# Residual updates of a SwiGLU down projection: by VectorE out of PSUM, in place of ScalarE copies and accumulating DMAs

## The chip, the cores and the metric

The kernel runs on one core of one Trainium2 chip. The metric is the device time of one launch in microseconds (us). The engines are named TensorE (PE in the profile), VectorE (DVE), ScalarE (ACT), GpSimd (POOL) and SyncE (SP). Each has its own instruction queue, worked through in order; semaphores tie the queues together. PEld is TensorE's weight load, which overlaps the matmul before it. PSUM has eight banks of 512 fp32 columns on 128 partitions.

## What is computed

One decoder layer on x (256 tokens, 2048 channels), fp32. Cut to what matters here:

```python
def swiglu(h, w_gate, w_up, w_down):
    return (jax.nn.silu(h @ w_gate) * (h @ w_up)) @ w_down

x = x + 0.5 * swiglu(rmsnorm(x, norm_ffn1), w1_gate, w1_up, w1_down)   # D_FF = 5632
h = rmsnorm(x, norm_mix); z = h @ w_in
x = x + concat(o_mla(z), o_rwkv(z)) @ w_out       # attention and RWKV-7 heads
x = x + 0.5 * swiglu(rmsnorm(x, norm_ffn2), w2_gate, w2_up, w2_down)
x = x + sigmoid(rmsnorm(x, norm_ple) @ w_ple_gate) * (p @ w_ple_proj)
```

The change touches the two SwiGLU blocks (f = 0 and f = 1).

## The kernel before

Every fp32 product is made of three fast products: each operand is split into a high part and the remainder, and hi\*hi, hi\*lo and lo\*hi are summed in PSUM. For a weight block `n` (1 MB, `raw[n % 3]`), ScalarE rounds it to `whi[n % 3]` (`split_hi`, L422), then VectorE subtracts to get `wlo[n % 2]` (`split_lo`, L431). SyncE loads block n + 3 into the same `raw` slot once `wlo` of block n is written (`load_unit`, L405, for gate and up; `load_block`, L396, for down).

A SwiGLU block goes through its 5632 hidden columns in 11 groups of 512. Ten passes (i = 0 to 9) each work on 12 weight blocks, numbered here u0 to u7 and d0 to d3:

- u0 to u7 are gate and up products for the next group of columns (`pe_units`). The even ones are plain products (L538 to L540, 24 matmuls). The odd ones use a seven-product scheme for the gate, which needs sums of weights `T` (`weight_forms` on VectorE, L443, L446, L448), their high part `t_hi` (`forms_hi` on ScalarE, L453) and their low part `t_lo` (`forms_lo` on VectorE, L458); 21 matmuls each (L555 to L557).
- d0 to d3 are the down products of the group that is ready (`down`, L471 to L473): four chunks of 512 output columns, 24 matmuls each, chunk j into banks 2j and 2j + 1. A pass has 4\*24 + 4\*21 + 4\*24 = 276 matmuls.
- At the end of the u blocks VectorE combines the gate and up sums (`combine_gate`, L801 to L808; `combine_up`, L813, L816), ScalarE applies silu (L676), VectorE makes h (`hidden`, L822) and turns it in quads (`h_turn`, L830). h then makes a trip through DRAM (`store_h`, `load_hT`) and comes back transposed for the next pass's down products.

The order on each engine is written out by hand: `pe_pass`, `act_pass`, `dve_pass` go through 12 steps s, and each step lists what stands in it. In `dve_pass`, step 9 ends with `split_lo` of d2, step 10 with `split_lo` of d3, step 11 has `split_lo` of the next pass's u0 and then `weight_forms` of the next u1. Passes 1 to 8 run as a hardware loop (L661, L780, L938); pass 9 stands behind it, and a last group of down products behind that.

The result of chunk j leaves PSUM so. ScalarE copies the two banks, times 0.5, into a buffer `xs[j % 2]` (`down_out`, L722) in steps 9, 10, 11 and, for chunk 3, step 0 of the next pass. GpSimd then issues a DMA that adds `xs` to `x` (`pool_add_x`, L1437), 80 in all. `xs` has two buffers, so the copy of chunk j waits for the add of chunk j - 2 (`x_added`). Before the next pass uses the banks, TensorE waits for the copies: `pe_pass` waits for chunk 2 before the first product (L634), `pe_units` for chunk 3 before the thirteenth (L568). The eleventh group's four chunks are added straight from the banks by VectorE (`last_out`, `update_x`, L850).

Of the kernel before, what the change touches and what calls it, by code (L numbers as in the profile page):

```python
# [11 lines left out]
ALU = mybir.AluOpType  # L12
ACT = mybir.ActivationFunctionType
# [3 lines left out]
P = 128  # L17
# [143 lines left out]
def hybrid_layer(nc, table, w, out):  # L161
    where = constant_table()[1]
    ctx = ExitStack()
    with ctx:
# [62 lines left out]
        t_hi = sb("t_hi", [P, WEIGHT_FORMS, COLS], F32R)  # L227
        more_hi = sb("more_hi", [P, SEVEN, 3 * P], F32R)
        more_lo = sb("more_lo", [P, SEVEN, 3 * P], F32R)
        XS0 = base[0]  # L230
        xs = sb("xs", [P, 2, TT, COLS])
        tok = sb("tok", [P, TT, TOKEN_FORMS, P], at=XS0)
        h_quads = sb("h_quads", [P, 4, FKT, TT, 32])


# [111 lines left out]
        h_dram = nc.dram_tensor("h_scratch", [P, TT * COLS], F32, kind="Internal").ap()  # L347
        tok_ready, tok_hi, tok_lo = map(sem, ("tok_ready", "tok_hi", "tok_lo"))
        p_done, s1_ready, combined = map(sem, ("p_done", "s1_ready", "combined"))
        x_evac, x_added = sem("x_evac"), [sem(f"x_added{k}") for k in range(2)]  # L350
        vec, pool_chain, zero_row = sem("vec"), sem("pool_chain"), sem("zero_row")
        z_evac, lora_stored, zero_stored = sem("z_evac"), sem("lora_stored"), sem("zero_stored")
        z_stored, z_shifted = sem("z_stored"), sem("z_shifted")
# [205 lines left out]
        def pe_units(pe, f, i, it):  # L559

            n = FFN_BASE[f] + PAIRS + 12 * i
            for v in range(PAIRS):
                m = n + v
                pe.wait_ge(lo_ready, m + 1 + 12 * it)
                if v % 2 == 0:
                    for out in (OUT_11, OUT_21, OUT_12, OUT_22):
                        if v == 0 and out == OUT_12 and i:
                            pe.wait_ge(x_evac, evacs(f, i - 1, 3) + 4 * it)  # L568
                        for kk in range(2):
                            ins = eight_products(m, out, kk, v == 0 and kk == 0, v == 6 and out == OUT_22 and kk == 1)  # L570
                    ins.then_inc(block_used, 1)
                    continue
                first, last = v == 1, v == 7
                if (i, v) == (0, 1):
                    pe.wait_ge(h_ready, NFF * f + 1)
                if i == 0:
                    pe.wait_ge(tok_lo, SEVEN * f + pair_of(m) + 1)
                ins = seven_product(m, P1, False, first, last)
                if last:
                    ins.then_inc(p_done, 1)  # L580
# [17 lines left out]
        def down(pe, f, i, it=0, last=False, turn_next=False):  # L598
            n = FFN_BASE[f] + PAIRS + 12 * i + (0 if last else PAIRS)
            h_hi, h_lo = (last_hT_hi, last_hT_lo) if last else (hT_hi, hT_lo)  # L600
            for j in range(4):
                if j == 0:
                    pe.wait_ge(hT_ready, NFF * f + i + 1 + it)
                if turn_next and j == 2:
                    pe.wait_ge(x_evac, evacs(f, i, 0))
                    last_h_turn(pe, f)
                if last:
                    if j < 2:
                        pe.wait_ge(x_evac, evacs(f, i - 1, 2 + j))
                    else:  # L610
                        pe.wait_ge(banks_read, (READ_OUT, READ_GATE)[f] - 4 + j - 1)
                    banks = (4 + 2 * (j % 2), 5 + 2 * (j % 2))
                else:
                    if j == 0:
                        pe.wait_ge(s1_ready, (NFF - 1) * f + i + 1 + it)
                    pe.wait_ge(combined, steps(f, i, (1, 2, 4, 5)[j]) + 5 * it)
                    banks = (2 * j, 2 * j + 1)
                products(pe, n + j, h_hi, h_lo, range(FKT), [banks], COLS, True, True, it)
                if last and j >= 2:
                    turn_x(pe, 2 * f + 1, (2 * j - 4, 2 * j - 3))  # L620
# [10 lines left out]

        def pe_pass(pe, f, i, it=0, turn_next=False):
            if i:
                pe.wait_ge(x_evac, evacs(f, i - 1, 2) + 4 * it)  # L634
            pe_units(pe, f, i, it)
            down(pe, f, i, it, turn_next=turn_next)

# [75 lines left out]
            act.wait_ge(p_done, 4 * ((NFF - 1) * f + i) + 1 + 4 * it)  # L713
            nc.scalar.activation(s1[:, :], PS[:, 0, :], ACT.Copy).then_inc(s1_ready, 1)

        def down_out(act, f, i, j, it=0):

            act.wait_ge(block_used, FFN_BASE[f] + PAIRS + 12 * i + PAIRS + j + 1 + 12 * it)
            adds = 2 * ((NFF - 1) * f + i) + j // 2
            if adds:  # L720
                act.wait_ge(x_added[j % 2], 16 * adds + 32 * it)
            nc.scalar.activation(xs[:, j % 2, :, :], PS[:, 2 * j:2 * j + 2, :], ACT.Copy, scale=0.5).then_inc(x_evac, 1)  # L722

        def token_hi(act, f, p):

            act.wait_ge(tok_ready, SEVEN * f + p + 1)
# [13 lines left out]
        def act_pass(act, f, i, it=0, turn_next=False):  # L740

            n = FFN_BASE[f] + PAIRS + 12 * i
            for s in range(12):
                if s == 0 and i:
                    down_out(act, f, i - 1, 3, it)
                if s in (0, 2, 4, 6):
                    forms_hi(act, n + s + 1, it)
                if s == 7:
                    first_sum(act, f, i, it)
                if s == 8:  # L750
                    silu(act, f, i, it)
                if s >= 9:
                    down_out(act, f, i, s - 9, it)
                split_hi(act, n + s + 2, it)
                if s == 4:
                    hT_part_hi(act, f, i, it)
                if s == 3 and not i:
                    token_hi(act, f, 3)
                if i == 0 and s in (1, 2):
                    (store_h, load_hT)[s - 1](act, f, 0)  # L760
                if not turn_next and s in (9, 10):
                    (store_h, load_hT)[s - 9](act, f, i + 1, it)
                if turn_next and s == 10:
                    last_hT_part_hi(act, f)

        def act_ffn(act, f, B):
# [13 lines left out]
            with act.Fori(0, NFF - 3) as it:  # L780
                act_pass(act, f, 1, it)
            act_pass(act, f, NFF - 2, turn_next=True)
            down_out(act, f, NFF - 2, 3)
            for s in range(4):
                split_hi(act, B + FFN_BLOCKS - 4 + s + 2)
            xT_parts_hi(act, 2 * f + 1, range(4))
# [56 lines left out]
            nc.vector.tensor_tensor(last_hT_lo[:, :, :].rearrange(banks, b=2), PS[:, 0:2, :],  # L843
                                    f32(last_hT_hi[:, :, :]).rearrange(banks, b=2), ALU.subtract).then_inc(hT_ready, 1)

        def update_x(dve, n, j, factor, it=0):

            dve.wait_ge(block_used, n + 1 + 12 * it)
            b = 4 + 2 * (j % 2)
            nc.vector.scalar_tensor_tensor(x[:, :, j * COLS:(j + 1) * COLS], PS[:, b:b + 2, :], factor,  # L850
                                           x[:, :, j * COLS:(j + 1) * COLS], ALU.mult, ALU.add).then_inc(banks_read, 1)

        def last_out(dve, f, B, j):
            dve.wait_ge(x_added[j % 2], 32 * (NFF - 1) * (f + 1) - 16 * (j < 2))
# [34 lines left out]
        def dve_pass(dve, f, i, it=0, turn_next=False):  # L889

            n = FFN_BASE[f] + PAIRS + 12 * i
            for s in range(12):
                if s == 8:
                    combine_up(dve, f, i, it)
                if i or s:
# [13 lines left out]
                if s == 8:  # L909
                    hidden(dve, f, i, it)  # L910
                    if not turn_next:
                        h_turn(dve, f, i + 1, it)
                if turn_next and s == 10:
                    last_hT_part_lo(dve, f)

        def dve_ffn(dve, f, B):
# [510 lines left out]
            pool_tt(pool, zst[:, :, :], zst[:, :, :], pvst[:, :, :], ALU.add)  # L1427
            pool.dma_start(z_dram[1:SEQ + 1, c:c + COLS].rearrange("(t p) c -> p t c", p=P), zst[:, :, :]).then_inc(z_stored, 16)

        def pool_add_x(pool, f):  # L1430

            for i in range(NFF - 1):
                for j in range(4):
                    pool.wait_ge(x_evac, evacs(f, i, j))
                    if i:
                        pool.wait_ge(x_added[j % 2], 16 * (2 * ((NFF - 1) * f + i - 1) + j // 2 + 1))
                    pool.dma_start(x[:, :, j * COLS:(j + 1) * COLS], xs[:, j % 2, :, :], accum_op=ALU.add).then_inc(  # L1437
                        x_added[j % 2], 16)

        def pool_aux(pool):  # L1440

            pool.wait_ge(con_loaded, 16)
# [2 lines left out]
            pool.dma_start(z_dram[0, :].rearrange("(p c) -> p c", p=P), zeros[:, :]).then_inc(zero_stored, 16)  # L1445
            pool.wait_ge(var_ready, 1)
            power(rstd[:, 0:2], "minus_half", rstd_ready)
            pool_add_x(pool, 0)
# [790 lines left out]
        def _(pool):  # L2239
# [10 lines left out]
            for k in range(2):  # L2250
                pool.wait_ge(var_ready, 5 + k)
                power(rstd[:, 4 + 2 * k:6 + 2 * k], "minus_half", rstd_ready)
                if k == 0:
                    pool_add_x(pool, 1)

        @block.tensor
        def _(pe):
# [93 lines left out]
        def _(dve):  # L2351
# [5 lines left out]
            for j in range(4):  # L2357
                for s in range(4):
                    if 4 * j + s >= 2:
                        split_lo(dve, WOUT + 4 * j + s + 1)  # L2360
                    if 4 * j + s == 9:
                        dve.wait_ge(p_hi, 1)
                        nc.vector.tensor_tensor(hT_lo[:, 0:2, :], PS[:, 0, :].rearrange("p (k s) -> p k s", k=2), f32(hT_hi[:, 0:2, :]),
                                                ALU.subtract).then_inc(p_ready, 1)
                update_x(dve, WOUT + 4 * j + 3, j, 1.0)
            split_lo(dve, PROJ + 1)
            xT_parts_lo(dve, 2, range(2))
            split_lo(dve, PROJ + 2)
# [47 lines left out]
```

## Time and profile before

| | us |
|---|---|
| median of 3 runs | 2008.17 (2005.13 to 2008.56) |
| profiled execution, its time | 2011.02 |
| profiled execution, its span | 2009.2 |
| PE busy | 1968.8 (98%) |
| DVE busy | 1522.9 (76%) |
| ACT busy | 1069.9 (53%) |
| POOL busy | 235.4 (12%) |

The profile is one execution; 1.8 us of its time lie outside the span. Busy shares are averages over the whole program. The granted TensorE clock was 0.997 of full speed.

### The profile page before, as it was taken

How to read it: one execution, taken by the hardware profiler on the slowest of the kernel's cores; microseconds unless marked ns; L12 is line 12 of the kernel's file. 1: busy time of each engine (PE TensorE's matmuls, PEld its weight loads, DVE VectorE, ACT ScalarE, POOL GpSimd, SP SyncE). 2: the span in 40 equal slices, each digit the busy share in tenths (PEclk: the TensorE clock that was granted, in tenths of full speed). 3: DMA queues.
4: the chain of work that ended last, by engine and by line, in shares of the span. 5: the costliest groups of instructions: out<-in, count | busy, mean ns of one | idle time of the engine just before them, and what ended most of it. 6: DMA issues, size and time to landing. Idle time of an engine off the chain costs nothing.

```text
span 2009.2 us, 28838 instructions
## 1 busy us (share of the span) xinstructions
PE 1968.8 (98%) x11016; PEld 1619.8 (81%) x11016; DVE 1522.9 (76%) x1364; ACT 1069.9 (53%) x1043; POOL 235.4 (12%) x190
## 2 busy tenths in 40 slices
PE   8999999999999999999898999999999999999999
PEld 6778778888888889888777888778887888887887
DVE  5978888788787855756788547977888888887664
ACT  4655555555554555855344346555555555555553
POOL 0000000000000000344533000000000000000000
PEclk9999999999999999999999999999999999999999
DMA  7688788877888766667312555688877888788854
GB/s 248 210 253 242 233 250 254 251 238 235 257 261 252 224 178 221 195 188 228 119 45 71 173 188 169 217 261 253 250 233 227 271 251 241 238 251 252 242 176 147
DMA packets 229035, 436.67 MB, mean 217 GB/s; under 512 B 12806, under 2 KB 32898, under 8 KB 228956
## 3 DMA queue, kind: packets, MB, share of 16 engines
q1 hardware_dynamic: 189116, 361.48, 53.7%
q0 software_dynamic: 25440, 53.09, 13.4%
q10 hardware_dynamic: 14400, 20.98, 3.1%
q8 instruction: 57, 0.93, 0.2%
q14 instruction: 22, 0.18, 0.0%
HBM read 374.42 MB, written 16.00 MB: 194 GB/s over the span
## 4 chain that ended last, share of the span: by engine, by line
PE 79%; DVE 10%; DMA 7%; ACT 2%; issue 2%; SPq 0%; DVEq 0%; ACTq 0%
PE PS L471 13%; PE PS L472 13%; PE PS L473 13%; DMA raw<-in_w_gate 7%; PE PS L538 6%; PE PS L540 6%; PE PS L539 6%; PE PS L555 5%; PE PS L556 5%; PE PS L557 5%; PE PS L1684 3%; DVE wlo L431 3%; DVE t_lo L458 2%; ACT t_hi L453 2%; DVE T L443 1%
## 5 line engine op out<-in xcount | busy, mean ns | idle before, releaser
L431 DVE TENSOR_TENSOR wlo<-raw,whi 128x2048 fp32r<-128x2048 f32 (+2 forms) x338 | 733.1, 2169 | 265.6 <-PE PS L473 246.2
L422 ACT ACTIVATE whi<-raw 128x2048 fp32r<-128x2048 f32 (+2 forms) x338 | 603.5, 1791 | 256.5 <-PE PS L473 143.8
L538 PE MATMUL PS<-whi,xT_hi 128*128 128x512 f32 x768 | 302.5, 394 | 5.0 <-issue 3.2
L540 PE MATMUL PS<-whi,xT_lo 128*128 128x512 f32 x768 | 300.5, 391 | 0.0
L539 PE MATMUL PS<-wlo,xT_hi 128*128 128x512 f32 x768 | 299.6, 390 | 0.0
L471 PE MATMUL PS<-whi,hT_hi 128*128 128x512 f32 x680 | 267.7, 394 | 1.5 <-DVE G L801 1.0
L473 PE MATMUL PS<-whi,hT_lo 128*128 128x512 f32 x680 | 265.0, 390 | 0.0
L472 PE MATMUL PS<-wlo,hT_hi 128*128 128x512 f32 x680 | 264.9, 390 | 0.0
L453 ACT ACTIVATE t_hi<-T 128x2048 fp32r<-128x2048 f32 x80 | 153.4, 1917 | 196.6 <-DVE T L448 196.6
L1437 POOL DMA_DIRECT2D x_resid<-xs x80 | 96.1, 1202 | 1195.2 <-ACT xs L722 1168.8
L458 DVE TENSOR_TENSOR t_lo<-T,t_hi 128x2048 fp32r<-128x2048 f32 x80 | 183.3, 2292 | 53.0 <-ACT t_hi L453 53.0
L471 PE MATMUL PS<-whi,xT_hi 128*128 128x512 f32 (+2 forms) x536 | 206.3, 385 | 0.0
L473 PE MATMUL PS<-whi,xT_lo 128*128 128x512 f32 (+2 forms) x536 | 203.4, 379 | 0.0
L472 PE MATMUL PS<-wlo,xT_hi 128*128 128x512 f32 (+2 forms) x536 | 203.3, 379 | 0.0
L722 ACT ACTIVATE xs<-PS 128x1024 f32<-128x1024 f32 x80 | 82.2, 1028 | 205.9 <-PE PS L473 142.1
L538 PEld LDWEIGHTS PS<-whi,xT_hi 128*128 128x128 f32 x768 | 144.5, 188 | 38.7 <-issue 6.7
L540 PEld LDWEIGHTS PS<-whi,xT_lo 128*128 128x128 f32 x768 | 144.6, 188 | 31.6
L539 PEld LDWEIGHTS PS<-wlo,xT_hi 128*128 128x128 f32 x768 | 144.7, 188 | 30.6
L471 PEld LDWEIGHTS PS<-whi,hT_hi 128*128 128x128 f32 x680 | 127.6, 188 | 34.9 <-DVE wlo L431 4.6
L473 PEld LDWEIGHTS PS<-whi,hT_lo 128*128 128x128 f32 x680 | 127.7, 188 | 27.4
L472 PEld LDWEIGHTS PS<-wlo,hT_hi 128*128 128x128 f32 x680 | 127.7, 188 | 26.0
L443 DVE TENSOR_TENSOR T<-raw 128x1024 f32<-128x1024 f32 x80 | 97.6, 1221 | 40.7 <-DMA raw<-in_w_gate 40.7
(384 smaller groups left out, 2776.4 us busy)
## 6 DMA issues: line engine op xcount, KB each, us to landing
raw<-in_w_up SPq DMA_DIRECT2D x176, 512.0 KB, 5.5
raw<-in_w_gate SPq DMA_DIRECT2D x176, 512.0 KB, 6.5
raw<-in_w_down SPq DMA_DIRECT2D x88, 1024.0 KB, 5.1
x_resid<-xs POOLq DMA_DIRECT2D x80, 512.0 KB, 9.4
raw<-in_w_in SPq DMA_DIRECT2D x28, 1024.0 KB, 5.7
raw<-in_w_out SPq DMA_DIRECT2D x16, 1024.0 KB, 5.1
raw<-in_w_ple_gate SPq DMA_DIRECT2D x16, 1024.0 KB, 5.2
h_scratch<-h_quads ACTq DMA_DIRECT2D x20, 512.0 KB, 5.9
```

The lines of the kernel that those rows point to most:

```text
L422: nc.scalar.activation(whi[:, n % WHI, a:wd], raw[:, n % RAW, a:wd], ACT.Copy).then_inc(hi_ready, 1)
L431: nc.vector.tensor_tensor(wlo[:, n % WLO, a:wd], raw[:, n % RAW, a:wd], f32(whi[:, n % WHI, a:wd]), ALU.subtract).then_inc(lo_ready, 1)
L443: nc.vector.tensor_tensor(T[:, 0:2, :], src[:, 1:3, :], src[:, 0:1, :].broadcast_to([P, 2, COLS]), ALU.subtract).then_inc(t_pair, 1)
L453: nc.scalar.activation(t_hi[:, :, :], T[:, :, :], ACT.Copy).then_inc(t_hi_ready, 1)
L458: nc.vector.tensor_tensor(t_lo[:, :, :], T[:, :, :], f32(t_hi[:, :, :]), ALU.subtract).then_inc(t_lo_ready, 1)
L471: nc.tensor.matmul(acc, a, whi[:, n % WHI, c], start=st, stop=False)
L472: nc.tensor.matmul(acc, a, wlo[:, n % WLO, c], start=False, stop=False)
L473: ins = nc.tensor.matmul(acc, b, whi[:, n % WHI, c], start=False, stop=en)
L538: nc.tensor.matmul(PS[:, bank, :], a, whi[:, n % WHI, c], start=first, stop=False)
L539: nc.tensor.matmul(PS[:, bank, :], a, wlo[:, n % WLO, c], start=False, stop=False)
L540: return nc.tensor.matmul(PS[:, bank, :], b, whi[:, n % WHI, c], start=False, stop=last)
L555: nc.tensor.matmul(PS[:, bank, :], a, hi, start=first, stop=False)
```

## The change

`down_out` moves from ScalarE to VectorE, and becomes a multiply-add: x = 0.5 \* banks + x, the operation of `update_x`. The buffer `xs`, the 80 copies and the 80 adding DMAs are gone, and so are the waits for `x_added`. TensorE now waits for `x_updated`, which VectorE raises, where it waited for `x_evac`. h still goes through DRAM. The diff, cut to its core:

```diff
-        XS0 = base[0]
-        xs = sb("xs", [P, 2, TT, COLS])
-        tok = sb("tok", [P, TT, TOKEN_FORMS, P], at=XS0)
+        tok = sb("tok", [P, TT, TOKEN_FORMS, P])
...
         def pe_pass(pe, f, i, it=0, turn_next=False):
             if i:
-                pe.wait_ge(x_evac, evacs(f, i - 1, 2) + 4 * it)
+                pe.wait_ge(x_updated, evacs(f, i - 1, 2) + 4 * it)
...
-        def down_out(act, f, i, j, it=0):
-
-            act.wait_ge(block_used, FFN_BASE[f] + PAIRS + 12 * i + PAIRS + j + 1 + 12 * it)
-            adds = 2 * ((NFF - 1) * f + i) + j // 2
-            if adds:
-                act.wait_ge(x_added[j % 2], 16 * adds + 32 * it)
-            nc.scalar.activation(xs[:, j % 2, :, :], PS[:, 2 * j:2 * j + 2, :], ACT.Copy, scale=0.5).then_inc(x_evac, 1)
...
@@ act_pass
-                if s == 0 and i:
-                    down_out(act, f, i - 1, 3, it)
-                if s >= 9:
-                    down_out(act, f, i, s - 9, it)
...
-        def update_x(dve, n, j, factor, it=0):
+        def update_x(dve, n, j, factor, banks, done, it=0):
 
             dve.wait_ge(block_used, n + 1 + 12 * it)
-            b = 4 + 2 * (j % 2)
-            nc.vector.scalar_tensor_tensor(x[:, :, j * COLS:(j + 1) * COLS], PS[:, b:b + 2, :], factor,
-                                           x[:, :, j * COLS:(j + 1) * COLS], ALU.mult, ALU.add).then_inc(banks_read, 1)
+            nc.vector.scalar_tensor_tensor(x[:, :, j * COLS:(j + 1) * COLS], PS[:, banks[0]:banks[1] + 1, :], factor,
+                                           x[:, :, j * COLS:(j + 1) * COLS], ALU.mult, ALU.add).then_inc(done, 1)
+
+        def down_out(dve, f, i, j, it=0):
+            update_x(dve, FFN_BASE[f] + PAIRS + 12 * i + PAIRS + j, j, 0.5, (2 * j, 2 * j + 1), x_updated, it)
...
@@ dve_pass
             for s in range(12):
+                if s == 0 and i:
+                    down_out(dve, f, i - 1, 3, it)
                 if s == 8:
                     combine_up(dve, f, i, it)
                 if i or s:
                     split_lo(dve, n + s + 1, it)
...
                 if s in (1, 3, 5) or (s == 11 and not turn_next):
                     weight_forms(dve, n + s + 2, it)
...
+                if s >= 9:
+                    down_out(dve, f, i, s - 9, it)
...
-        def pool_add_x(pool, f):
-
-            for i in range(NFF - 1):
-                for j in range(4):
-                    pool.wait_ge(x_evac, evacs(f, i, j))
-                    if i:
-                        pool.wait_ge(x_added[j % 2], 16 * (2 * ((NFF - 1) * f + i - 1) + j // 2 + 1))
-                    pool.dma_start(x[:, :, j * COLS:(j + 1) * COLS], xs[:, j % 2, :, :], accum_op=ALU.add).then_inc(
-                        x_added[j % 2], 16)
```

How this moves the instructions, at two places. First VectorE, from the end of pass 0 into pass 1. Before (the three L431 split d2, d3 and the next u0, and the L431 after the branch splits the next u1):

```order
L830 STREAM_TRANSPOSE h_quads<-h 128x4x4x32
L431 TENSOR_TENSOR wlo<-raw,whi 128x2048 [waits block_used,hi_ready] x3
L443 TENSOR_TENSOR T<-raw 128x1024 [waits raw_loaded0,t_lo_ready]
L446 TENSOR_TENSOR T<-T,raw 128x512 [waits t_pair]
L448 TENSOR_TENSOR T<-T,raw 128x512 [waits t_third]
L938 UNCONDITIONAL_BRANCH
L938 ISA
L430 REGISTER_ALU [waits hi_ready]
L431 TENSOR_TENSOR wlo<-raw,whi 128x1536 [waits block_used]
```

and after:

```order
L429 TENSOR_TENSOR wlo<-raw,whi 128x2048 [waits block_used,hi_ready]
L834 SCALAR_TENSOR_TENSOR x_resid<-PS,x_resid 128x2x512 [waits block_used]
L429 TENSOR_TENSOR wlo<-raw,whi 128x2048 [waits block_used,hi_ready]
L834 SCALAR_TENSOR_TENSOR x_resid<-PS,x_resid 128x2x512 [waits block_used]
L429 TENSOR_TENSOR wlo<-raw,whi 128x2048 [waits block_used,hi_ready]
L441 TENSOR_TENSOR T<-raw 128x1024 [waits raw_loaded0,t_lo_ready]
L444 TENSOR_TENSOR T<-T,raw 128x512 [waits t_pair]
L446 TENSOR_TENSOR T<-T,raw 128x512 [waits t_third]
L834 SCALAR_TENSOR_TENSOR x_resid<-PS,x_resid 128x2x512 [waits block_used]
L928 UNCONDITIONAL_BRANCH
L928 ISA
L834 SCALAR_TENSOR_TENSOR x_resid<-PS,x_resid 128x2x512 [waits block_used]
```

The update of chunk 0 stands behind the split of d2, that of chunk 1 behind the split of d3, that of chunk 2 behind the split of u0 and the three instructions of `weight_forms`, and that of chunk 3 at the head of the next pass, ahead of the split of u1.

Second ScalarE, in the same stretch, from the split of u0's predecessor d3 to the high part of u1's weight sums. Before:

```order
L722 ACTIVATE xs<-PS 128x1024 [waits block_used]
L422 ACTIVATE whi<-raw 128x2048 [waits block_used,raw_loaded2]
L708 DMA hT<-h_scratch 32x4x256 [waits h_stored]
L708 DMA hT<-h_scratch 32x4x256 x3
L722 ACTIVATE xs<-PS 128x1024 [waits x_added0,block_used]
L422 ACTIVATE whi<-raw 128x1536 [waits block_used,raw_loaded0]
L780 UNCONDITIONAL_BRANCH
L780 ISA
L721 ISA [waits block_used]
L722 ACTIVATE xs<-PS 128x1024 [waits x_added1]
L451 ISA
L453 ACTIVATE t_hi<-T 128x2048 [waits block_used,t_ready]
```

and after:

```order
L420 ACTIVATE whi<-raw 128x2048 [waits block_used,raw_loaded2]
L706 DMA hT<-h_scratch 32x4x256 [waits h_stored]
L706 DMA hT<-h_scratch 32x4x256 x3
L420 ACTIVATE whi<-raw 128x1536 [waits block_used,raw_loaded0]
L766 UNCONDITIONAL_BRANCH
L766 ISA
L450 ISA [waits t_ready]
L451 ACTIVATE t_hi<-T 128x2048 [waits block_used]
```

The copies, and their waits for the adding DMAs, are gone from between ScalarE's splits; nothing else changed its order.

## Rows read from the trace of the kernel before

**Rows 1.** The page: span, busy time by engine, and the chain that ended last.

```profile
span 2009.2 us, 28838 instructions
PE 1968.8 (98%) x11016; PEld 1619.8 (81%) x11016; DVE 1522.9 (76%) x1364; ACT 1069.9 (53%) x1043; POOL 235.4 (12%) x190
...
PE 79%; DVE 10%; DMA 7%; ACT 2%; issue 2%; SPq 0%; DVEq 0%; ACTq 0%
```

**Rows 2.** Timeline, VectorE, `combine_gate`: start, duration, engine, line, operation.

```profile
103.59 1.22 DVE L801 TENSOR_TENSOR G<-PS,s 128x1024 f32<-128x1024 f32 x1
167.85 1.23 DVE L801 TENSOR_TENSOR G<-PS,s 128x1024 f32<-128x1024 f32 x1
232.87 1.22 DVE L801 TENSOR_TENSOR G<-PS,s 128x1024 f32<-128x1024 f32 x1
297.31 1.23 DVE L801 TENSOR_TENSOR G<-PS,s 128x1024 f32<-128x1024 f32 x1
...
551.93 1.23 DVE L801 TENSOR_TENSOR G<-PS,s 128x1024 f32<-128x1024 f32 x1
615.04 1.23 DVE L801 TENSOR_TENSOR G<-PS,s 128x1024 f32<-128x1024 f32 x1 [0.37 <-PE PS L557]
678.78 1.23 DVE L801 TENSOR_TENSOR G<-PS,s 128x1024 f32<-128x1024 f32 x1 [0.25 <-PE PS L557]
...
1292.45 1.22 DVE L801 TENSOR_TENSOR G<-PS,s 128x1024 f32<-128x1024 f32 x1
...
1867.11 1.23 DVE L801 TENSOR_TENSOR G<-PS,s 128x1024 f32<-128x1024 f32 x1 [0.25 <-PE PS L557]
```

**Rows 3.** Waits, TensorE's weight loads, 90 to 750 us: total, times, longest (us).

```profile
PEld PS L555 <- DVE t_lo L458: 5.8, 9, 0.8
PEld PS L555 <- DVE wlo L431: 3.0, 4, 1.4
```

**Rows 4.** Groups by line and shape: count, busy us and mean ns, idle us before.

```profile
L722 ACT ACTIVATE xs<-PS 128x1024 f32<-128x1024 f32 x80 | 82.2, 1028 | 205.9 <-PE PS L473 142.1 <-DMA x_resid<-xs 41.3 <-issue 22.5
L850 DVE SCALAR_TENSOR_TENSOR x_resid<-PS,x_resid 128x1024 f32<-128x1024 f32 x12 | 14.7, 1221 | 16.0 <-PE PS L473 16.0
```

**Rows 5.** Timeline, VectorE, from one pass into the next.

```profile
310.47 2.29 DVE L431 TENSOR_TENSOR wlo<-raw,whi 128x2048 fp32r<-128x2048 f32 x1 [1.06 <-PE PS L473]
315.91 2.29 DVE L431 TENSOR_TENSOR wlo<-raw,whi 128x2048 fp32r<-128x2048 f32 x1 [3.15 <-PE PS L473]
318.12 1.22 DVE L443 TENSOR_TENSOR T<-raw 128x1024 f32<-128x1024 f32 x1
...
320.10 0.69 DVE L448 TENSOR_TENSOR T<-T,raw 128x512 f32<-128x512 f32 x1
...
331.90 1.23 DVE L443 TENSOR_TENSOR T<-raw 128x1024 f32<-128x1024 f32 x1 [1.41 <-DMA raw<-in_w_gate]
...
333.89 0.69 DVE L448 TENSOR_TENSOR T<-T,raw 128x512 f32<-128x512 f32 x1
334.50 1.75 DVE L431 TENSOR_TENSOR wlo<-raw,whi 128x1536 fp32r<-128x1536 f32 x1
```

**Rows 6.** Timeline, TensorE, matmuls: first of d3, and first of the next u0.

```profile
315.64 0.39 PE L471 MATMUL PS<-whi,hT_hi 128*128 128x512 f32 x1
...
321.08 0.39 PE L538 MATMUL PS<-whi,xT_hi 128*128 128x512 f32 x1
```

**Rows 7.** Timeline, VectorE and TensorE, a wait for a late `wlo`.

```profile
206.73 1.75 DVE L431 TENSOR_TENSOR wlo<-raw,whi 128x1536 fp32r<-128x1536 f32 x1
...
207.14 0.39 PE L540 MATMUL PS<-whi,xT_lo 128*128 128x512 f32 x1
208.53 0.50 PE L555 MATMUL PS<-whi,xT_hi 128*128 128x512 f32 x1 [1.01 <-DVE wlo L431]
208.87 0.40 PE L556 MATMUL PS<-wlo,xT_hi 128*128 128x512 f32 x1
```

**Rows 8.** DMA, 304 to 330 us: packets, MB, share of 16 engines' time.

```profile
q0 software_dynamic: 966, 1.88, 39.5%
```

More of the change, by code:

```diff
@@ L349, in hybrid_layer @@
         p_done, s1_ready, combined = map(sem, ("p_done", "s1_ready", "combined"))
-        x_evac, x_added = sem("x_evac"), [sem(f"x_added{k}") for k in range(2)]
+        x_updated = sem("x_updated")
         vec, pool_chain, zero_row = sem("vec"), sem("pool_chain"), sem("zero_row")
@@ L567, in pe_units @@
                         if v == 0 and out == OUT_12 and i:
-                            pe.wait_ge(x_evac, evacs(f, i - 1, 3) + 4 * it)
+                            pe.wait_ge(x_updated, evacs(f, i - 1, 3) + 4 * it)
                         for kk in range(2):
@@ L604, in down @@
                 if turn_next and j == 2:
-                    pe.wait_ge(x_evac, evacs(f, i, 0))
+                    pe.wait_ge(x_updated, evacs(f, i, 0))
                     last_h_turn(pe, f)
@@ L608, in down @@
                     if j < 2:
-                        pe.wait_ge(x_evac, evacs(f, i - 1, 2 + j))
+                        pe.wait_ge(x_updated, evacs(f, i - 1, 2 + j))
                     else:
@@ L782, in act_ffn @@
             act_pass(act, f, NFF - 2, turn_next=True)
-            down_out(act, f, NFF - 2, 3)
             for s in range(4):
@@ L844, in last_hT_part_lo @@
                                     f32(last_hT_hi[:, :, :]).rearrange(banks, b=2), ALU.subtract).then_inc(hT_ready, 1)
-        def update_x(dve, n, j, factor, it=0):
+        def update_x(dve, n, j, factor, banks, done, it=0):
             dve.wait_ge(block_used, n + 1 + 12 * it)
-            b = 4 + 2 * (j % 2)
-            nc.vector.scalar_tensor_tensor(x[:, :, j * COLS:(j + 1) * COLS], PS[:, b:b + 2, :], factor,
-                                           x[:, :, j * COLS:(j + 1) * COLS], ALU.mult, ALU.add).then_inc(banks_read, 1)
+            nc.vector.scalar_tensor_tensor(x[:, :, j * COLS:(j + 1) * COLS], PS[:, banks[0]:banks[1] + 1, :], factor,
+                                           x[:, :, j * COLS:(j + 1) * COLS], ALU.mult, ALU.add).then_inc(done, 1)
+        def down_out(dve, f, i, j, it=0):
+            update_x(dve, FFN_BASE[f] + PAIRS + 12 * i + PAIRS + j, j, 0.5, (2 * j, 2 * j + 1), x_updated, it)
         def last_out(dve, f, B, j):
-            dve.wait_ge(x_added[j % 2], 32 * (NFF - 1) * (f + 1) - 16 * (j < 2))
-            update_x(dve, B + FFN_BLOCKS - 4 + j, j, 0.5)
+            update_x(dve, B + FFN_BLOCKS - 4 + j, j, 0.5, (4 + 2 * (j % 2), 5 + 2 * (j % 2)), banks_read)
         def token_sums(dve, f, p):
@@ L940, in dve_ffn @@
             dve_pass(dve, f, NFF - 2, turn_next=True)
+            down_out(dve, f, NFF - 2, 3)
             split_lo(dve, B + FFN_BLOCKS - 3)
@@ L1447, in pool_aux @@
             power(rstd[:, 0:2], "minus_half", rstd_ready)
-            pool_add_x(pool, 0)
             pool.wait_ge(var_ready, 2)
@@ L2252, in _ @@
                 power(rstd[:, 4 + 2 * k:6 + 2 * k], "minus_half", rstd_ready)
-                if k == 0:
-                    pool_add_x(pool, 1)
         @block.tensor
@@ L2364, in _ @@
                                                 ALU.subtract).then_inc(p_ready, 1)
-                update_x(dve, WOUT + 4 * j + 3, j, 1.0)
+                update_x(dve, WOUT + 4 * j + 3, j, 1.0, (4 + 2 * (j % 2), 5 + 2 * (j % 2)), banks_read)
             split_lo(dve, PROJ + 1)
```

## The prediction

> **What bounds the kernel now.** I read the page first, then the timeline of one line that comes once a pass, then the waits, then the timelines of the two engines across the border between two passes.
>
> The page puts TensorE at 1968.8 us busy of 2009.2, and 79% of the chain that ended last on it, with VectorE 10% and DMA 7% [rows 1]. So TensorE sets the time, and what others can win is the time TensorE waits for them. How much that is in the passes shows in the starts of `combine_gate`, one a pass [rows 2]. From pass 0 to pass 9 of the first SwiGLU they are 678.78 - 103.59 = 575.19 us apart, of the second 1867.11 - 1292.45 = 574.66: nine intervals each, 18 in all, 1149.85 us. The shortest that I found is 615.04 - 551.93 = 63.11 us; I take it as a pass in which nobody is late. 276 matmuls in it are 0.2287 us each. The other intervals are longer, up to 232.87 - 167.85 = 65.02. The excess over 18 shortest ones is 1149.85 - 18 * 63.11 = 1149.85 - 1135.98 = 13.9 us. The waits name it: the weight loads of the odd u blocks wait for `t_lo` (9 times, 5.8 us in the first SwiGLU) and for `wlo` (4 times, 3.0 us) [rows 3]. VectorE makes both.
>
> Why VectorE is late, I read from its timeline [rows 5]. It isn't short of time over the pass: it sat idle 3.15 us before the split of u0, waiting for TensorE. It is late after a late load: the T of u3 waited 1.41 us for its weights and began at 331.90, and from there VectorE works without a gap (to 333.89 and 334.50), so the lateness is handed on to `wlo` and `t_lo` of u3.
>
> **What the change removes.** The 80 copies on ScalarE, 1.028 us each, 82.2 us [rows 4]. ScalarE isn't on the path there: it idled 205.9 us before them. I take 0 for this. The waits for the adds that stood in the copies, 41.3 us, go too [rows 4]; one of them stood ahead of the high part of u1's sums, which only starts u1's `t_lo` sooner, and u1 isn't where TensorE waited. 0 again. The 80 adding DMAs matter more. Between 304 and 330 us, where the loads of u1 to u3 are under way, the GpSimd queue's packets took 39.5% of the 16 DMA engines' time, 0.395 * 26 = 10.3 us [rows 8]. That time comes free exactly ahead of the load for which the T of u3 waited 1.41 us [rows 5]. So I expect that wait to go, and with it the start of the lateness.
>
> By the Trainium skill, "SBUF — State Buffer", in the part on who interferes with whom, VectorE's hold on a shared port can keep GpSimd from writing the descriptors of its DMAs, so that such a DMA starves while the DMA engines idle. By that rule the adds would be slow without costing the loads much, and taking them out would bring the loads little; the sum would then be the one of the second rival below. The trace speaks against it here, since that queue's packets did take their share of the engines.
>
> **What the change adds.** 80 multiply-adds on VectorE. `update_x` does the same operation on the same shape in the last group: 1.221 us [rows 4]. 80 * 1.22 = 97.7 us, 4.9 us a pass. As a share of VectorE's time this fits: 1522.9 + 97.7 = 1620.6 of 2009. What counts is where each stands.
>
> Chunk 0 follows the split of d2. The split of d3 starts when TensorE has done d1; before, VectorE idled 1.06 us ahead of it [rows 5]. The update overlaps its neighbours by some 0.1 us as VectorE's instructions do (T starts 2.21 us after a split of 2.29), so 1.14 us go into a gap of 1.06: at most 0.1 us late for a block that TensorE wants 10 us later. Cost 0. Chunk 1 follows the split of d3, into the idle 3.15 us. Cost 0.
>
> Chunk 2 is the dear one. TensorE's first product of the next u0 waits for it, and it stands behind the split of u0 and the whole of `weight_forms`. I count from the start s of the split of u0, which TensorE itself releases (end of d2), so that s is tied to TensorE's own time. On the row s = 315.91 [rows 5]. The last instruction of `weight_forms` starts at 320.10, s + 4.19. It takes 0.69, and the next independent one starts 0.61 after it (333.89 to 334.50 on the rows): s + 4.80. The update takes 1.22: s + 6.02. TensorE wants to start u0 at 321.08, s + 5.17 [rows 6]. What a late release costs is seen where `wlo` of u1 was late [rows 7]: VectorE ended at 206.73 + 1.75 = 208.48, the first matmul started at 208.53 (0.05 later) and the second at 208.87, 0.34 after the first. Undisturbed, matmuls follow each other by (321.08 - 315.64)/24 = 0.227 us [rows 6]. So after the change the second matmul of u0 starts at s + 6.02 + 0.05 + 0.34 = s + 6.41, and would have started at s + 5.17 + 0.23 = s + 5.40. **The price is 1.01 us at each border between passes.** Borders are 9 in each SwiGLU (0 to 1, up to 8 to 9), 18 in all: 18 * 1.01 = 18.2 us. Behind pass 9 there is no `weight_forms` in that step, so chunk 2 is ready by about s + 2.2 + 1.2 = s + 3.4, ahead of s + 5.17: cost 0 there.
>
> Chunk 3 comes next on VectorE, at about s + 5.9 to 7.2. TensorE needs it before its 13th matmul of u0, at s + 6.41 + 11 * 0.227 = s + 8.9. Cost 0. Behind it are queued the split of u1 and `t_lo` of u1. The split of u1 would run from s + 7.1 to s + 8.8, and TensorE needs it a block of 24 matmuls after its late start, at about s + 6.1 + 5.4 = s + 11.5; cost 0. The load of u4 waits for that split and goes out some 1.7 us later than before; it has the time that the adds leave free as its cover, and if that were gone, u4 to u7 would pass on up to 1.7 us.
>
> **What is won back.** The 13.9 us are lateness of VectorE against TensorE at u1 and u3 and, once, elsewhere. Two things work on it. The loads come earlier, as said. And TensorE itself starts each u0 1.01 us later, so VectorE is 1.01 us less late even if no load comes earlier. In the first SwiGLU three intervals exceed 63.11 + 1.01 = 64.12: 64.26, 65.02 and 64.44 [rows 2], by 0.14, 0.90 and 0.32, together 1.4 us. With the same for the second, only about 2.7 us of the 13.9 could survive without faster loads, and none with them. I take none, since 10.3 us of DMA time stand against a wait of 1.41.
>
> **The sum.** +18.2 - 13.9 = +4.3 us. Against the profiled execution: span 2009.2 + 4.3 = 2013.5, time 2015.3. That execution was 2.9 us above the median of the runs shown, so against the median it is 2008.2 + 4.3 = **2012.5 us**. The two large terms nearly cancel; each is known to perhaps 2 us (0.1 us a border, 0.1 us a pass).
>
> **The rivals.** (1) Loads don't come earlier. Then 2.7 us of lateness stay: +7.0, 2015.2 us. For it: SyncE issues the loads when VectorE frees a slot, and those times hardly move. Against it: the share of the adds [rows 8].
>
> (2) Nothing is won back, because chunk 3 ahead of the split of u1 and the later load of u4 keep VectorE as late as it was, against a TensorE that has moved. Then +18.2: 2026.4 us. For it: the gapless run from 331.90 on [rows 5]. Against it: that run starts when a load lands, not when VectorE is free.
>
> (3) Not slower: the matmuls themselves get quicker. At the border they follow by 0.227 us, over the shortest pass by 0.2287 on average, so a pass holds 63.11 - 276 * 0.2267 = 0.5 us in which TensorE is a little slower than its best without a named wait. If that is the DMA or PSUM traffic of the copies and adds, the change takes it away: 18 * 0.54 = 9.7 us, sum -5.4, 2002.8 us. It decides the sign from 4.3/18 = 0.24 us a pass on. For it: two engines no longer work on chunk results at once. Against it: the best pace of 0.227 stands just where the adds were under way (315 to 321 us) [rows 6, 8].
>
> (4) The wait for chunk 2 is hidden. If TensorE lost less than 13.9/18 = 0.77 us at a border instead of 1.01, the sum would be nil or a gain. That needs the update to start 0.24 us earlier than the rows allow; it can't overtake `weight_forms`. It would give 2008 us or less.
>
> **How the numbers follow.** Forecast 0.55, (1) 0.13, (2) 0.07, (3) 0.12, (4) 0.13. A measurement of this kernel can tell about 0.2%, 4 us, from no change: slower means above 2012.2, faster below 2004.2. The forecast itself straddles the upper bound, with some 0.2 of its 0.55 below it; with (4) and a part of (3) that makes 0.37 for no change. Faster has most of (3), 0.08. Slower has the rest, 0.55. The range goes from 2007, which leaves out (3), to 2018, which holds (1) with its 2 us and leaves out (2).
>
> **What would show it.** In the profile after, the first weight load of u0 should wait for `x_resid` by VectorE, 18 times, about 1.2 us each (a weight load's wait shows some 0.2 more than it costs). The T of u3 should no longer wait for a load, and the waits for `t_lo` and `wlo` of odd u blocks should be gone or nearly. Intervals of `combine_gate` should all be near 63.11 + 1.01 = 64.1 us, with little scatter. The GpSimd queue should carry nothing in the passes. I am wrong if the border wait is below 0.8 or above 1.3 us, if late `t_lo` stays beside it, or if VectorE's durations or the pace of the matmuls change.

## The result and the profile after

Median of 5 runs 2018.81 us (2016.05 to 2024.0), against 2006.34 us of the kernel before (2005.13 to 2008.56, 5 runs). The ratio is 1.0063, with a 95% interval of 1.0045 to 1.008. In a second comparison, further down, it was 1.0055 (1.004 to 1.007), 2017.96 against 2007.99 us. So the change costs 10 to 12.5 us. The prediction had the direction, slower by more than 0.2%, but its 2012.5 us and the top of its range, 2018, lie below the measured 2018.81; the 2017.96 of the second comparison lies just under that top.

The page of the kernel after, span, busy time and chain, answers to [rows 1]:

```profile
span 2016.8 us, 28552 instructions
PE 1966.0 (97%) x11016; PEld 1619.0 (80%) x11016; DVE 1613.4 (80%) x1444; ACT 997.8 (49%) x963; POOL 139.6 (7%) x110
...
PE 85%; DVE 9%; issue 4%; ACT 1%; DMA 1%; DVEq 0%; SPq 0%; ACTq 0%
```

VectorE is busy 90.5 us longer (80 updates, each taking the next instruction's start 1.14 us further, are 91), and TensorE is still the engine that sets the time. DMA fell from 7% of the chain to 1%; "issue" rose from 2% to 4%. What stands behind "issue", the last rows of this section show.

The starts of `combine_gate`, one a pass, answer to [rows 2] (columns as there; this kernel's L786 is L801 of before):

```profile
104.71 1.22 DVE L786 TENSOR_TENSOR G<-PS,s 128x1024 f32<-128x1024 f32 x1
170.17 1.23 DVE L786 TENSOR_TENSOR G<-PS,s 128x1024 f32<-128x1024 f32 x1 [0.45 <-PE PS L555]
234.39 1.23 DVE L786 TENSOR_TENSOR G<-PS,s 128x1024 f32<-128x1024 f32 x1 [0.45 <-PE PS L555]
...
555.58 1.23 DVE L786 TENSOR_TENSOR G<-PS,s 128x1024 f32<-128x1024 f32 x1 [0.45 <-PE PS L555]
619.81 1.23 DVE L786 TENSOR_TENSOR G<-PS,s 128x1024 f32<-128x1024 f32 x1 [0.45 <-PE PS L555]
683.97 1.23 DVE L786 TENSOR_TENSOR G<-PS,s 128x1024 f32<-128x1024 f32 x1 [0.45 <-PE PS L555]
...
1296.52 1.22 DVE L786 TENSOR_TENSOR G<-PS,s 128x1024 f32<-128x1024 f32 x1
...
1874.63 1.23 DVE L786 TENSOR_TENSOR G<-PS,s 128x1024 f32<-128x1024 f32 x1 [0.45 <-PE PS L555]
```

The scatter of before is gone: 619.81 - 555.58 = 64.23, and 16 of the 18 intervals lie between 64.15 and 64.25. The first of each SwiGLU is longer, 65.46 and 64.31. Together they are 579.26 + 578.11 = 1157.37 us, 7.5 more than in the profile of before, and the spans differ by 2016.8 - 2009.2 = 7.6. Outside these intervals the two profiles differ by 1.1 us twice, with opposite signs (pass 0 starts 1.12 us later, the stretch between the SwiGLUs is 1.12 us shorter), so the net difference is that of the passes. VectorE now waits 0.45 us for TensorE before each `combine_gate` but the first of a SwiGLU ([0.45 <-PE PS L555]): it isn't late there any more.

Where VectorE's lateness began, at T, the wait for loads (groups by line; idle us before), before and then after:

```profile
L443 DVE TENSOR_TENSOR T<-raw 128x1024 f32<-128x1024 f32 x80 | 97.6, 1221 | 40.7 <-DMA raw<-in_w_gate 40.7
L441 DVE TENSOR_TENSOR T<-raw 128x1024 f32<-128x1024 f32 x80 | 97.5, 1219 | 1.1 <-DMA raw<-in_w_gate 1.1
```

One wait of 1.1 us is left, at the first border, in place of 20 waits in 20 passes. The loads themselves land sooner (DMA issues: KB each, median us from issue to landing), before and then after:

```profile
raw<-in_w_gate SPq DMA_DIRECT2D x176, 512.0 KB, 6.5
raw<-in_w_gate SPq DMA_DIRECT2D x176, 512.0 KB, 4.8
```

The border itself, VectorE and then TensorE (timelines), answers to [rows 5] and [rows 6]:

```profile
574.19 2.29 DVE L429 TENSOR_TENSOR wlo<-raw,whi 128x2048 fp32r<-128x2048 f32 x1 [2.01 <-PE PS L471]
576.40 1.22 DVE L441 TENSOR_TENSOR T<-raw 128x1024 f32<-128x1024 f32 x1
...
578.38 0.69 DVE L446 TENSOR_TENSOR T<-T,raw 128x512 f32<-128x512 f32 x1
578.99 2.35 DVE L834 SCALAR_TENSOR_TENSOR x_resid<-PS,x_resid 128x1024 f32<-128x1024 f32 x2
581.25 1.75 DVE L429 TENSOR_TENSOR wlo<-raw,whi 128x1536 fp32r<-128x1536 f32 x1
```

```profile
579.13 0.39 PE L471 MATMUL PS<-whi,hT_lo 128*128 128x512 f32 x1
580.34 0.49 PE L536 MATMUL PS<-whi,xT_hi 128*128 128x512 f32 x1 [0.82 <-DVE x_resid L834]
580.67 0.39 PE L537 MATMUL PS<-wlo,xT_hi 128*128 128x512 f32 x1
```

With s = 574.19, T starts at s + 2.21, the last instruction of `weight_forms` at s + 4.19, the updates of chunks 2 and 3 at s + 4.80: each as worked out ahead. Two updates back to back take 2.35 us, so the first ends 1.22 in, at s + 6.02. TensorE's last matmul of d3 starts at 579.13; the first of u0 could have followed at 579.36 and came at 580.34, the second came at 580.67, s + 6.48, where s + 6.41 was predicted. The difference lies in the release: 580.34 - 580.21 = 0.13 us from VectorE's end to the matmul (0.12 to its weight load), not 0.05. In the pass behind the loop the same step is 644.49 - 644.44 = 0.05:

```profile
643.22 2.35 DVE L834 SCALAR_TENSOR_TENSOR x_resid<-PS,x_resid 128x1024 f32<-128x1024 f32 x2
...
644.49 0.50 PE L536 MATMUL PS<-whi,xT_hi 128*128 128x512 f32 x1 [0.74 <-DVE x_resid L834]
```

In the loop the value waited for depends on the loop's counter (`+ 4 * it`); behind the loop it is a constant. And in the loop the profile puts the weight load's idle time down to issue and not to VectorE:

```profile
580.33 0.19 PEld L536 LDWEIGHTS PS<-whi,xT_hi 128*128 128x128 f32 x1 [1.24 <-issue]
```

Whether that form of the wait is what takes the 0.07 us more, no run here separates. The 18 borders are alike: the first matmul of u0 idles 0.81 or 0.82 us in the loop and 0.74 behind it, but for the 1.97 at the first border, where a load was late. Of the signs named ahead, the wait at each border (its weight load idle 1.16 to 1.24 us, and 2.39 at the first), the missing wait for loads and the intervals near 64.1 came true; of late `t_lo` one wait of 0.6 us is left.

### The profile page after: what moved, and what is told of

The parts are those of the page before. It is cut to its first block, busy times and chain, and to the rows that moved or that the text cites. A ratio compares the mean times of both kernels' runs of the same rounds, so it can differ in the third digit from the quotient of the medians.

```text
span 2016.8 us, 28552 instructions
## 1 busy us (share of the span) xinstructions
PE 1966.0 (97%) x11016; PEld 1619.0 (80%) x11016; DVE 1613.4 (80%) x1444; ACT 997.8 (49%) x963; POOL 139.6 (7%) x110
## 4 chain that ended last, share of the span: by engine, by line
PE 85%; DVE 9%; issue 4%; ACT 1%; DMA 1%; DVEq 0%; SPq 0%; ACTq 0%
PE PS L469 12%; PE PS L471 12%; PE PS L470 12%; PE PS L536 8%; PE PS L538 8%; PE PS L537 8%; PE PS L553 6%; PE PS L554 6%; PE PS L555 6%; PE PS L1664 2%; DVE wlo L429 2%; DVE T L441 2%; DVE x_resid L834 1%; DVE T L444 1%; PE PS L490 1%
## 5 line engine op out<-in xcount | busy, mean ns | idle before, releaser
L538 PEld LDWEIGHTS PS<-whi,xT_lo 128*128 128x128 f32 x768 | 144.7, 188 | 32.1
L834 DVE SCALAR_TENSOR_TENSOR x_resid<-PS,x_resid 128x1024 f32<-128x1024 f32 x92 | 110.5, 1217 | 19.7 <-PE PS L471 19.7
L1149 POOL TENSOR_TENSOR rstd<-rstd,con 128x2 f32<-128x2 f32 x6 | 8.2, 1375 | 1575.7 <-DVE rstd L1144 1575.7
L471 PEld LDWEIGHTS PS<-whi,xT_lo 128*128 128x128 f32 x536 | 100.7, 188 | 18.7
```

Of the source, the lines that this page charges most:

```text
L471: ins = nc.tensor.matmul(acc, b, whi[:, n % WHI, c], start=False, stop=en)
L538: return nc.tensor.matmul(PS[:, bank, :], b, whi[:, n % WHI, c], start=False, stop=last)
```

## The experiments

The theory: TensorE loses about 1.1 us at each of 18 borders, because the update of chunk 2 stands behind `weight_forms`; the freed DMA time takes VectorE's lateness away; and the error of the prediction lies in how much lateness there was to win. The rivals: VectorE has no room for the updates wherever they stand; the lateness was VectorE's own and not the traffic's; something else than chunk 2 sets the border's price; ScalarE's copies, or their waits for the adds, made the lateness, and not the adds' traffic.

The table compares all profiles by the starts of `combine_gate` (pass 0 and 9 of each SwiGLU). "18 intervals" is their sum, "excess" that sum less 18 * 63.14 us, the interval that the quiet kernels below settled on. The times behind the profiles come from three comparisons, each with runs of the kernel before beside it (medians 2006.34, 2007.99 and 2006.91 us). "Between" is from pass 9 of the first SwiGLU to pass 0 of the second, which the change doesn't touch.

| profile of | first SwiGLU | second SwiGLU | 18 intervals | excess | between | its time |
|---|---|---|---|---|---|---|
| before | 103.59 to 678.78 | 1292.45 to 1867.11 | 1149.85 | 13.3 | 613.67 | 2011.02 |
| before, second profile | 103.66 to 677.91 | 1290.38 to 1862.74 | 1146.61 | 10.1 | 612.47 | 2006.65 |
| before, third profile | 104.55 to 678.27 | 1290.11 to 1861.75 | 1145.36 | 8.8 | 611.84 | 2005.65 |
| after | 104.71 to 683.97 | 1296.52 to 1874.63 | 1157.37 | 20.9 | 612.55 | 2018.81 |
| after, second profile | 103.67 to 681.85 | 1299.02 to 1877.22 | 1156.38 | 19.9 | 617.17 | 2021.3 |
| chunk 2 ahead | 104.47 to 672.73 | 1285.24 to 1853.49 | 1136.51 | 0.0 | 612.51 | 1997.63 |
| before without adds | 104.88 to 673.16 | 1284.88 to 1853.13 | 1136.53 | 0.0 | 611.72 | 1997.03 |
| after with traffic | 104.53 to 683.17 | 1294.62 to 1873.62 | 1157.64 | 21.1 | 611.45 | 2017.85 |
| chunk 2 ahead, with traffic | 103.32 to 678.15 | 1291.97 to 1861.81 | 1144.67 | 8.1 | 613.82 | 2006.08 |
| after with a longer queue | 104.28 to 687.48 | 1301.38 to 1884.57 | 1166.39 | 29.9 | 613.90 | 2028.48 |

**Chunk 2 ahead of `weight_forms`.** One call in `dve_pass` is moved.

```diff
                 if s == 4 and not i:
                     token_lo(dve, f, 3)
+                if s >= 9:
+                    down_out(dve, f, i, s - 9, it)
                 if s in (1, 3, 5) or (s == 11 and not turn_next):
                     weight_forms(dve, n + s + 2, it)
...
-                if s >= 9:
-                    down_out(dve, f, i, s - 9, it)
```

> The changed kernel with one thing moved: in step 11 the update of chunk 2 stands ahead of weight_forms instead of behind it. Theory A (the price is the place of chunk 2 in VectorE's order): chunk 2 is ready by about s + 3.4 us, ahead of TensorE's s + 5.17, the 18 waits for x_resid at the borders go, and with them 18 * 1.09 us and the longer wait at the first border; intervals of combine_gate near 63.15 us, about 1998 us, 0.4% less than the kernel before. Rival B (VectorE has no room for the updates, wherever they stand): the T of u1 is 1.14 us later, t_lo or wlo of u1 is late instead, the time stays within 5 us of the changed kernel, 2014 to 2019.

Measured: 1997.89 us (1996.23 to 2002.31, 6 runs), ratio to the kernel before 0.9956 (0.9941 to 0.9972). It is 20 us faster than the changed kernel and beats the kernel before as well. Its border (timelines):

```profile
565.05 2.29 DVE L429 TENSOR_TENSOR wlo<-raw,whi 128x2048 fp32r<-128x2048 f32 x1 [2.01 <-PE PS L471]
567.26 1.22 DVE L834 SCALAR_TENSOR_TENSOR x_resid<-PS,x_resid 128x1024 f32<-128x1024 f32 x1
568.39 1.22 DVE L441 TENSOR_TENSOR T<-raw 128x1024 f32<-128x1024 f32 x1
...
570.98 1.22 DVE L834 SCALAR_TENSOR_TENSOR x_resid<-PS,x_resid 128x1024 f32<-128x1024 f32 x1
572.11 1.75 DVE L429 TENSOR_TENSOR wlo<-raw,whi 128x1536 fp32r<-128x1536 f32 x1
573.78 2.28 DVE L456 TENSOR_TENSOR t_lo<-T,t_hi 128x2048 fp32r<-128x2048 f32 x1
```

```profile
569.99 0.39 PE L471 MATMUL PS<-whi,hT_lo 128*128 128x512 f32 x1
570.22 0.39 PE L536 MATMUL PS<-whi,xT_hi 128*128 128x512 f32 x1
```

Chunk 2 is done at 567.26 + 1.22 = 568.48, 1.74 us before TensorE starts u0 at 570.22, with no gap behind d3's last matmul. T, pushed back by 1.13 us, delays nobody. All 18 intervals lie between 63.11 and 63.20. This settles that VectorE has the room: the 4.9 us of work a pass cost nothing but for the one place in the order.

**The kernel before without its adding DMAs.** ScalarE still copies; GpSimd issues nothing; x lacks the down products of ten groups in each SwiGLU.

```diff
-            adds = 2 * ((NFF - 1) * f + i) + j // 2
-            if adds:
-                act.wait_ge(x_added[j % 2], 16 * adds + 32 * it)
+            if evacs(f, i, j) > 1:
+                act.wait_ge(x_evac, evacs(f, i, j) - 1 + 4 * it)
...
-            dve.wait_ge(x_added[j % 2], 32 * (NFF - 1) * (f + 1) - 16 * (j < 2))
...
-            pool_add_x(pool, 0)
...
-                if k == 0:
-                    pool_add_x(pool, 1)
```

> The kernel before without its 80 adding DMAs; ScalarE still copies into xs, which is left there, so x misses the down products of ten groups in each SwiGLU. Theory A (the adds' traffic makes the loads of u1 to u3 late, and these make VectorE late): intervals of combine_gate near 63.15 us with no scatter, waits for t_lo and wlo of odd blocks gone, 8 to 13 us less than the kernel before, 1994 to 1998 us. Rival B (lateness is VectorE's own): within 3 us of the kernel before, 2004 to 2009.

Measured: 1997.66 us (1996.88 to 2000.97), ratio 0.9957 (0.9942 to 0.9972). The intervals are those of the kernel above, 63.12 to 63.18. The gate loads land in 4.6 us (median; 6.5 with the adds). All of the lateness came with the adds, and ScalarE's copies, which are still there, cost nothing once nobody makes them wait. With the adds went ScalarE's waits for them too (41.3 us, [rows 4]), so this run alone doesn't say which of the two made TensorE late; the run with both edits below does for most of it. Of TensorE's own waits for a copy there were 2 or 3 in each profile of the kernel before, 0.4 to 0.8 us together. The waits of the weight loads on the odd blocks, 90 to 750 us, answer to [rows 3]; of the 13 waits for `t_lo` and `wlo` one is left:

```profile
PEld PS L555 <- DVE t_lo L458: 0.6, 1, 0.6
```

**The traffic put back into the changed kernel.** 80 adding DMAs of the same size, from a constant table into a buffer that nobody reads (`tok` now lies in it); its declaration, its zeroing and the waits for it are left out here. No engine but GpSimd waits for these adds. They are a little lighter than the real ones: 11520 packets in place of 21760, 8.5 us from issue to landing in place of 9.4 (medians).

```diff
...
+        def pool_traffic(pool, f):
+
+            pool.wait_ge(con_loaded, 16)
+            pool.wait_ge(ident_loaded, 16)
+            pool.wait_ge(tok_lo, SEVEN * (f + 1))
+            for i in range(NFF - 1):
+                for j in range(4):
+                    pool.wait_ge(x_updated, evacs(f, i, j))
+                    if f or i or j >= 2:
+                        pool.wait_ge(y_sent[j % 2], 16 * (2 * ((NFF - 1) * f + i) + j // 2))
+                    pool.dma_start(ys[:, (j % 2) * TT * COLS:(j % 2 + 1) * TT * COLS].rearrange("p (t c) -> p t c", t=TT), con[:, 0:TT * COLS].rearrange("p (t c) -> p t c", t=TT),
+                                   accum_op=ALU.add).then_inc(y_sent[j % 2], 16)
...
```

> The changed kernel with the traffic put back: GpSimd issues 80 adding DMAs of the same 512 KB, each when a chunk is updated, from a constant table into a buffer that nobody reads. If the loads' lateness hides behind the 1.09 us that TensorE loses at each border, only its excess shows: 1 to 4 us more than the changed kernel, 2019 to 2023, with some intervals above 64.24. If the lateness adds up in full (it was won back by the freed DMA time alone): 8 to 13 us more, 2027 to 2032. If the traffic didn't matter: no difference.

Measured: 2020.29 us (2017.85 to 2026.07), ratio 1.0071 (1.0055 to 1.0087). That is 2.3 us above the changed kernel of the same comparison (2017.96), with the intervals of the two ratios overlapping. In its profile the T waits for loads are back, 15.5 us in 12 waits, but only two intervals stand out, 64.75 and 65.04; the others are 64.17 to 64.29. So the lateness that this traffic brings hides almost wholly behind the wait at the border.

**Both: chunk 2 ahead, and the traffic.** The edits of the first and third experiment together.

> The update of chunk 2 ahead of weight_forms, and the 80 adding DMAs of traffic put back (from a constant table into a buffer that nobody reads). With no wait at the borders there is nothing behind which late loads can hide. Theory A (the traffic makes VectorE late, the borders' wait hid it in the changed kernel): waits for t_lo and wlo of u1 and u3 come back, intervals scatter from 63.1 to 65 us, 7 to 13 us more than with the update first alone, 2005 to 2011. Rival B (what was won back came from ScalarE's copies gone, not from the traffic): no scatter, 1997 to 2000.

Measured: 2008.11 us (2001.56 to 2012.44, 12 runs), ratio 1.0002 (0.9991 to 1.0013): 10.2 us above chunk 2 ahead alone (9.2 by the two ratios, since that ran in another comparison), and as slow as the kernel before. Its intervals scatter from 63.12 to 64.99. There are no copies in it, and ScalarE waits for no add: the traffic alone brings back 8.1 us of the 8.8 to 13.3. Whether the rest is the lighter traffic or ScalarE's waits isn't settled. The waits of VectorE name the origin (total, times, longest):

```profile
DVE T L442 <- DMA raw<-in_w_gate: 22.8, 16, 3.3
```

and TensorE's weight loads, 90 to 750 us, wait for what follows from it:

```profile
PEld PS L554 <- DVE t_lo L457: 4.2, 7, 0.8
PEld PS L537 <- DVE wlo L430: 4.1, 4, 1.4
```

The four runs with and without wait and traffic make a square: the border wait costs 20.1 us without traffic (2017.96 - 1997.89) and 12.2 with it (2020.29 - 2008.11); the traffic costs 10.2 us without the wait and 2.3 with it. Three of the four are of one comparison and the fourth of another; by the ratios to the kernel before, the 12.2 is 13.9, and the 18 intervals of the profiles give 20 to 21 and 13.0. Either way the two don't add up, since one hides the other.

**A longer queue ahead of chunk 2.** One more VectorE instruction of 480 elements, whose result is read by nobody (its declarations are left out here).

```diff
...
+                if s == 11 and not turn_next:
+                    pads = (NFF - 2) * f + i
+                    if pads:
+                        dve.wait_ge(padded, pads + it)
+                    dve.wait_ge(x_updated, evacs(f, i, 0) + 4 * it)
+                    nc.vector.tensor_tensor(pad[:, :], x[:, 0, 0:480], x[:, 1, 0:480], ALU.add).then_inc(padded, 1)
                 if s >= 9:
                     down_out(dve, f, i, s - 9, it)
```

> The changed kernel with one more VectorE instruction of 480 elements a partition in step 11, between weight_forms and the update of chunk 2; its result is read by nobody. Such an instruction of 512 elements moves the next by 0.61 us, this one by some 0.58. If TensorE's loss at a border is set by when VectorE reaches chunk 2, each border costs 0.58 more: intervals 64.24 + 0.58 = 64.82 us, 18 * 0.58 = 10.4 us more, 2028 to 2030. If something else sets it (the wait's own overhead, the release of the banks), the time stays at 2018.

Measured: 2028.9 us (2025.8 to 2029.95, 4 runs), ratio 1.0104 (1.0088 to 1.0121). The instruction pushes chunk 2 by 322.72 - 322.15 = 0.57 us:

```profile
322.15 0.65 DVE L907 TENSOR_TENSOR pad<-x_resid 128x480 f32<-128x480 f32 x1
322.72 2.35 DVE L835 SCALAR_TENSOR_TENSOR x_resid<-PS,x_resid 128x1024 f32<-128x1024 f32 x2
```

Fourteen of the 18 intervals are 64.80, 0.57 above 64.23. The price follows the queue ahead of chunk 2 one to one, so it is chunk 2's place in that queue that sets it.

**The changed kernel once more.**

> The changed kernel once more, unchanged, for a second profile and the spread of its runs: 2016 to 2021 us, intervals of combine_gate at 64.24 us but for the first of each SwiGLU, where the T of u1 can wait for its load.

Measured: 2017.96 us (2016.77 to 2021.45). The intervals are 64.18 to 64.32, and neither first one is long. The 65.46 of the first profile was one late load: there T of u1 waited 1.06 us, and since chunk 2 stands behind T, TensorE waited with it:

```profile
126.75 1.23 DVE L441 TENSOR_TENSOR T<-raw 128x1024 f32<-128x1024 f32 x1 [1.06 <-DMA raw<-in_w_gate]
```

The stretch between the SwiGLUs took 617.17 us here, against 612.55; its mean granted clock was 0.99 against 1.00. In both profiles the clock falls some 290 us into that stretch; in this one it stays low for 10 us more (0.69 of full speed on average from 991.85 to 1001.85 us, where the other had 1.00). But the first profile of the kernel before had 0.99 too and took 613.67, so the clock by itself doesn't give the 617.17, and what made it differ isn't settled.

**The kernel before, two more profiles.**

> The kernel before once more, unchanged, for a second profile of its lateness. The prediction took 13.9 us of it from one profile whose run was 3 us above the median. If that run was unusually late, the excess of the 18 intervals over 63.13 is smaller here, 7 to 11 us; if not, about 13 again.

> The same as the run before it, a third profile of the kernel before: excess of 7 to 11 us if the first profile was unusually late, about 13 if not.

Their starts of pass 9 in the second SwiGLU:

```profile
1862.74 1.23 DVE L801 TENSOR_TENSOR G<-PS,s 128x1024 f32<-128x1024 f32 x1 [0.23 <-PE PS L557]
```

```profile
1861.75 1.23 DVE L801 TENSOR_TENSOR G<-PS,s 128x1024 f32<-128x1024 f32 x1 [0.25 <-PE PS L557]
```

against 1867.11 in [rows 2]. The excess is 10.1 and 8.8 us, where the first profile had 13.3, and these executions took 2006.65 and 2005.65 us, close to the median. The T waits for loads follow it: 32.6 and 34.3 us, where the first had 40.7. The first profile was a late one.

## Why the prediction was wrong

**What bounds it, and what becomes late next: right.** TensorE sets the time; chunks 0, 1 and 3 cost nothing (with them in place and chunk 2 moved, the intervals are those of a kernel without updates in the passes); chunk 2 costs at each of 18 borders and nowhere else. The wait stands where it was put, with the timeline offsets predicted up to the end of the update.

**The price of a border: mis-sized by a tenth.** 1.01 us predicted, 1.10 measured (19.86 / 18, from the second profile of the changed kernel; the matmul rows show 1.08: 580.67 where 579.36 + 0.23 = 579.59 was due). 0.07 of the difference is the slower release, at the 16 borders in the loop; at the two behind it the interval is 64.16 and 64.15, the price 1.02. Over 18 borders that is 19.8 in place of 18.2, +1.6 us. The late load at the first border added 1.2 in the first profile (65.46 against 64.28), and isn't there in the other.

**Won back in full: right as a mechanism.** Without the adds no lateness is left: 18 intervals of 63.14 where chunk 2 is out of the way. The estimate of 63.11 for a quiet pass was 0.03 low, 0.5 us in the sum. The third experiment puts the first rival's case to the test, lateness from traffic beside the wait at the border: it was priced at 2.7 us more, and 2.3 was measured. So the greater part of the gain did not need the faster loads; the wait at the border hides most of such lateness by itself.

**The size of what is won back: this step failed.** "The excess over 18 shortest ones is ... 13.9 us" was read from one execution that took 2011.02 us, 2.9 us above the median then known and 4.7 above the 2006.34 of five runs. The sum then set it against the median: "against the median it is 2008.2 + 4.3". But the part by which that execution was slow was in good part the very lateness that the change takes away: it took 4.4 and 5.4 us more than the two other profiled ones, and its excess was 3.2 and 4.5 us larger (13.3 against 10.1 and 8.8). A median run has less of it to give. So the gain of one execution was taken off the time of another. Kept within one execution, the sum comes out: 2011.02 + 19.8 - 13.3 = 2017.5 us, against medians of 2018.81 and 2017.96. With the mean of the three profiles, 10.7, and the measured price, the sum is 19.8 - 10.7 = +9.1 us; the passes of the two kernels differ by 1156.9 - 1147.3 = +9.6 on the mean of their profiles, and the second comparison has +10.0. The first has +12.5, with an interval (1.0045 to 1.008, 9 to 16 us) that holds these. What makes up the further 2.5 us isn't settled; the stretch between the SwiGLUs, which the change leaves alone, scattered by 5.7 us over the profiles.

**The range failed with it.** Two large terms of opposite sign were each given 2 us. One of them had a spread of 4.5 us between executions, and one profile can't show that. The time of the profiled run against the median was a sign of it; it was used to shift the result to the median, and not to shrink the gain.

**The other rivals.** (2), nothing won back: no, as the intervals show. (3), quicker matmuls: no, the quiet pass is 63.14 with and without copies, and with the adds the shortest is 63.11 or 63.12. (4), the wait hidden: no; but the first experiment is its counterpart, with the update where it could be early. The prediction's remark that adds which cost the loads nothing would lead to the second rival points at the wrong one: that is the first rival's case, 2015.2 us. It didn't arise, since the loads land sooner without the adds.

## What to carry to other kernels

Before work is moved onto an engine that has room, look at what stands ahead of it in that engine's order and when its result is first wanted; one call moved by one place was worth 20 us here, more than the whole change. A wait that a change adds and a lateness that it takes away don't add up, since each can hide the other. And when a gain is read from one profile, ask whether that execution's distance from the median is made of the same thing; if so, the gain belongs to that execution and not to the median.

## What was not expected of the hardware

The release of TensorE by a semaphore took 0.12 us inside the hardware loop and 0.05 outside it, from the end of VectorE's instruction to the start of the weight load. And 80 adding DMAs of 512 KB from SBUF to SBUF were enough to bring 8.1 to 13.3 us of lateness into the passes. Over the whole program GpSimd's queue took 13.4% of the DMA engines' time with them and 2.0% without, so they took some 11%. In the passes (104 to 670 us) the DMA engines were 81% busy with the adds and 66% without. That mean hides that the loads of u1 to u3 come in one bunch, in which the adds fell too: between 304 and 330 us the gate loads landed in 11.0 us (median) with the adds, and in 5.4 without.
